# One block for router and experts, and a first expert round from the first four token tiles

## What is computed

```
x = x + g1 * mix                                  # output projection and residual
h = modulate(x, norm2_g, sh2, sc2)
lc = h @ router_c + b;  g_idx = argmax(lc)        # one of 4 groups
lf = h @ router_f + b;  lf_sel = the 4 values of that group
top_w, top_i = top_k(softmax(lf_sel), 2)          # two of its 4 experts
for e in range(16):
    hid = silu(h @ exp_gate[e]) * (h @ exp_up[e])
    out += combine[:, e] * (hid @ exp_down[e])
x = x + g2 * out
```

## Time and profile before

| | |
|---|---|
| three runs | 920.63, 917.87, 919.87 us, median 919.87 |
| profiled execution, span from first to last instruction | 917.0 us; its own time beside the span is not listed, the median of the runs lies 2.9 us above it |
| PE busy | 846.8 us, 92% |
| DVE, ACT, POOL busy | 47%, 27%, 8% |
| DMA, mean over the span | 249 GB/s |
| DMA in the slices from 596 us to 894 us | 304 to 425 GB/s a slice |
| mean granted PE clock | 0.958 of full |

### The profile page before, as it was taken

The page is one execution under the profiler, slowest core; times in us unless marked ns, Lnnn a source line. Parts: engine busy times, 40 slices in busy tenths (PEclk is TensorE's granted clock), DMA queues, the critical chain, the costliest instruction groups (busy, mean ns, idle before and its releaser), DMA issues. The chain is left out here.

```text
span 917.0 us, 18956 instructions
## 1 busy us (share of the span) xinstructions
PE 846.8 (92%) x8190; PEld 486.0 (53%) x8190; DVE 432.1 (47%) x878; ACT 249.9 (27%) x489; POOL 77.7 (8%) x126
## 2 busy tenths in 40 slices
PE   5999999999989987799988899928999999999998
PEld 4455555544656765688877555514344444333433
DVE  4321356222457877778885755661331000002248
ACT  5002222322588772323322302111111111111110
POOL 1180000000000002122211000120000000000040
PEclk9999999999999996899999799967999999999999
DMA  9989999573890001001322664299989999999993
GB/s 342 322 243 408 379 391 362 218 264 110 332 379 14 14 13 36 5 20 46 95 61 61 207 230 183 77 357 393 372 304 400 406 378 378 414 391 411 425 377 124
DMA packets 72612, 227.89 MB, mean 249 GB/s; under 512 B 10708, under 2 KB 15884, under 8 KB 66128
## 3 DMA queue, kind: packets, MB, share of 16 engines
q1 hardware_dynamic: 60784, 200.33, 58.6%
q10 hardware_dynamic: 7632, 14.64, 4.5%
q0 software_dynamic: 4112, 11.70, 3.8%
HBM read 166.98 MB, written 59.67 MB: 247 GB/s over the span
## 5 line engine op out<-in xcount | busy, mean ns | idle before, releaser
L2595 PE MATMUL ps<-arena 128*32 128x512 f32 (+2 forms) x800 | 170.2, 597 | 1.5 <-ACT arena L2730 1.5
L2595 PEld LDWEIGHTS ps<-arena 128*32 128x32 f32 (+2 forms) x800 | 61.3, 136 | 101.8 <-issue 99.1
L1012 PE MATMUL ps<-arena 128*128 128x128 f32 (+1 forms) x384 | 106.8, 435 | 0.0
L1012 PEld LDWEIGHTS ps<-arena 128*128 128x128 f32 x384 | 58.4, 190 | 50.6 <-issue 48.9
L2143 PE MATMUL ps<-arena 128*128 128x512 f32 x160 | 74.0, 615 | 1.9 <-PEq L1516 1.9
L2637 PE MATMUL ps<-arena 128*32 128x512 f32 (+2 forms) x352 | 70.6, 594 | 0.0
L748 DVE SCALAR_TENSOR_TENSOR arena<-arena 128x128 f32<-128x128 f32 (+3 forms) x56 | 30.9, 553 | 69.8 <-ACT arena L655 68.3
L2906 DVE TENSOR_TENSOR arena<-arena,ps 128x512 f32<-128x512 f32 x12 | 8.2, 687 | 100.3 <-ACT arena L2726 100.3
L891 PE MATMUL ps<-arena 128*128 128x512 f32 (+1 forms) x160 | 52.4, 486 | 0.0
L2143 PEld LDWEIGHTS ps<-arena 128*128 128x128 f32 x160 | 30.5, 197 | 37.3 <-issue 37.3
L2637 PEld LDWEIGHTS ps<-arena 128*32 128x32 f32 (+2 forms) x352 | 24.4, 132 | 38.7 <-issue 37.9
(11 more groups left out here) (395 smaller groups left out, 1315.1 us busy)
## 6 DMA issues: line engine op xcount, KB each, us to landing
gathered_tokens<-arena SPq DMA_DIRECT2D x16, 2560.0 KB, 21.2
arena<-in_exp_up_dram SPq DMA_DIRECT2D x16, 2048.0 KB, 20.8
arena<-in_exp_gate_dram SPq DMA_DIRECT2D x16, 2048.0 KB, 20.8
arena<-in_exp_down_dram SPq DMA_DIRECT2D x16, 2048.0 KB, 20.9
arena<-in_w_mod_dram SPq DMA_DIRECT2D x12, 2048.0 KB, 15.0
arena<-in_w_in_dram SPq DMA_DIRECT2D x4, 2048.0 KB, 12.5
expert_outputs<-arena ACTq DMA_DIRECT2D x10, 512.0 KB, 11.8
arena<-in_x_sample_dram SPq DMA_DIRECT2D x8, 512.0 KB, 9.1
```

Source lines behind the costliest of these rows:

```text
L1012: mm = pe.matmul(ps[:, b, 0:hi - lo], ring_of(what)[:, k, (e % 4) * P:(e % 4) * P + P], hT[:, k, lo:hi], start=(k == 0), stop=(k == KT - 1))
L2595: mm = pe.matmul(ps[c:c + m, b, :], xgT[:, k, c:c + m], w[n % 3][:, k, :], start=(k == 0), stop=(k == KT - 1))
```

## The change

The two blocks become one; each engine's two lists are joined. Besides:

- Round 0 takes 64 rows of each fixed place (two quarters and two quarters), round 1 the rest of both and the first quarter of place 2. Place 0 therefore stays until round 1. A round's results go to HBM in contiguous pieces (stretches), two each for rounds 0 and 1.
- Batches become tiles 0 to 2, tile 3, tile 4. After tile 3, the fixed experts' next row is set to at least 64 (first_rows), so that no row of tile 4 can fall in round 0.
- ACT loads round 0's rows when tiles 0 to 3 are scattered, in the middle of tile 4's routing; the rows of rounds 1 and 2 after tile 4's scatter and the table.
- PE turns round 0's rows ahead of the second half of tile 4's partial logits, and does tile 4's logits and ranks between the gate products of round 0.
- SP issues the gate weight of place 1 at attn_read, which PE sets when it has read the attention part of tile 4's projection; the down weight of place 1 follows the up weight; the weights of place 2 wait for the table, not for the block's end.
- DVE ranks the four values by comparing each with each (rank_of_four) in place of repeated maxima; the values for the softmax weights are made at the end (chosen_values).

```diff
-        SEGS = [[] for _ in range(NR)]
...
+        SEGS = [[(0, 0, 0, 2), (1, 2, 0, 2)], [(0, 0, 2, CAPQ[0] - 2), (1, CAPQ[0] - 2, 2, CAPQ[1] - 2)]] + [[] for _ in range(NR - 2)]
+        for n in range(len(FIXED), NE):
...
+        def stretches(r):
+            out = []
+            for n, c0, q0, nq in SEGS[r]:
+                at = QROWS * (sum(CAPQ[:n]) + q0)
+                if out and out[-1][1] + out[-1][2] == at:
+                    out[-1][2] += QROWS * nq
+                else:
+                    out.append([QROWS * c0, at, QROWS * nq])
+            return out
...
-        BATCHES = ((0, 2), (2, 4), (4, NTT))
+        BATCHES = ((0, 3), (3, 4), (4, NTT))
...
             @block.sync
             def _(sp):
...
-                sp.wait_ge(mix_mm, 2 * NTT - 1)
+                sp.wait_ge(attn_read, 1)
                 sp.dma_start(wg[1], exp_gate[0, FIXED[1]].rearrange("(p k) n -> p k n", p=P)).then_inc(ld_g[1], 16)
                 sp.wait_ge(mix_mm, 2 * NTT)
                 sp.dma_start(wu[1], exp_up[0, FIXED[1]].rearrange("(p k) n -> p k n", p=P)).then_inc(ld_u[1], 16)
-                sp.wait_ge(ld_g2b, 32)
+                sp.dma_start(wd[1], exp_down[0, FIXED[1]].rearrange("(p k) n -> p k n", p=P)).then_inc(ld_d[1], 16)
+                sp.wait_ge(h2_ok, NTT)
+                sp.wait_ge(table_ok, 1)
                 e = expert_at(sp, 2)
-                sp.dma_start(iota, consts[:, NCONST + 8 * C:]).then_inc(ld_iota, 16)
                 sp.dma_start(wg[2], gate_of(e)).then_inc(ld_g[2], 16)
                 sp.dma_start(wu[2], up_of(e)).then_inc(ld_u[2], 16)
-                sp.dma_start(wd[1], exp_down[0, FIXED[1]].rearrange("(p k) n -> p k n", p=P)).then_inc(ld_d[1], 16)
+                sp.dma_start(iota, consts[:, NCONST + 8 * C:]).then_inc(ld_iota, 16)
+                for b, (t0, t1) in enumerate(BATCHES):
+                    sp.wait_ge(scattered[b], 32 * (t1 - t0))
                 sp.dma_start(wd[2], down_of(e)).then_inc(ld_d[2], 16)
...
+                half_squares(4, 0)
+                act.wait_ge(scattered[0], 96)
+                act.wait_ge(scattered[1], 32)
+                load_rows(act, 0)
+                x2_turned(4, (0,))
+                half_squares(4, 1)
+                root_square(4)
+                x_out(0)
+                logits_out(4)
+                sigmoid(0)
+                act.wait_ge(scattered[2], 32)
+                act.wait_ge(table_ok, 1)
+                load_rows(act, 1)
+                load_rows(act, 2)
+                act.wait_ge(ec_ok, 1)
+                act.activation(expc, expc, ACT.Exp).then_inc(ex_ok, 1)
...
+                mix_half(4, 1, 0, (0, 1))
+                ranks(1)
+                mix_half(4, 1, 0, (2, 3))
+                pe.wait_ge(cat_ok, NTT)
+                mix_half(4, 0, 1)
+                mix_half(4, 1, 1)
+                x2_turn(4, (0,))
+                part_logits_of(4, (0,))
+                x2_turn(4, (1,))
...
                 x_turn(0)
-                gate_up(0)
+                part_logits_of(4, (1,))
+                pe.wait_ge(slot_ok, 2)
+                pe.wait_ge(xgT_ok, 1)
+                weights_landed(0, ld_g)
+                products(0, wg, GA, 0, 1)
+                logits_of(4)
+                products(0, wg, GA, 1, 5)
+                ranks(2)
+                products(0, wg, GA, 5, KT).then_inc(g6_mm, 1)
+                weights_landed(0, ld_u)
+                products(0, wu, UP, 0, KT).then_inc(u6_mm, 1)
                 x_turn(1)
                 h_turn(0)
+                pe.wait_ge(slot_ok, 3)
                 for r in range(1, NR):
...
+                def rank_of_four(n, ts, vals):
+                    for op, beside in ((ALU.is_equal, 0), (ALU.is_gt, 1)):
+                        ins = dve.tensor_tensor(beats[:, ts, :, beside], vals.unsqueeze(2).to_broadcast([P, n, 4, 4]),
+                                                vals.unsqueeze(3).to_broadcast([P, n, 4, 4]), op)
+                    ch(ins)
+                    ch(dve.tensor_tensor(beats[:, ts, :, 0], beats[:, ts, :, 0], earlier.unsqueeze(1).to_broadcast([P, n, 4, 4]), ALU.mult))
...
+                choose(1, *BATCHES[1])
+                place_rows(1)
+                ch(dve.tensor_tensor(offs[:, 4, 0:len(FIXED)], offs[:, 4, 0:len(FIXED)], first_rows, ALU.max))
```

More of the change, by code:

```diff
@@ L1947, in build, with stored_before @@
                 SEGS[r].append((n, lo - 4 * r, lo - at, hi - lo))
+        assert all(sum(nq for _, _, _, nq in one) == 4 for one in SEGS)
+        FIRST_ROUND = [min(r for r in range(NR) if n in [i for i, _, _, _ in SEGS[r]]) for n in range(NE)]
+        LAST_ROUND = [max(r for r in range(NR) if n in [i for i, _, _, _ in SEGS[r]]) for n in range(NE)]
+        def stretches(r):
[7 more added lines that the diff above has]
+            return out
+        def stored_before(r):
+            return 16 * sum(len(stretches(i)) for i in range(r))
         def load_rows(eng, r):
@@ L2513, in tiles_of @@
                 return [(0, P, SEGS[r][0][0])]
-            w = 64 if SEGS[r][0][3] == 2 else 32
+            w = 64 if all(nq == 2 for _, _, _, nq in SEGS[r]) else 32
             return [(QROWS * c, w, n) for n, c0, _, nq in SEGS[r] for c in range(c0, c0 + nq, w // QROWS)]
@@ new lines, in mix_half @@
+                def mix_half(tt, half, k4, js=range(NC4)):
+                    b = 2 + 2 * (tt % 2) + half
+                    for j in js:
+                        mm = pe.matmul(ps[:, b, :], catT[k4][:, j, tt * P:(tt + 1) * P], wout[:, half, NC4 * k4 + j, :],
+                                       start=(k4 == 0 and j == 0), stop=(k4 == 1 and j == NC4 - 1))
+                    if k4 and NC4 - 1 in js:
+                        mm.then_inc(mix_mm, 1)
+                    elif tt == NTT - 1 and half and NC4 - 1 in js:
+                        mm.then_inc(attn_read, 1)
@@ new lines, in _ @@
+                pe.wait_ge(ld_at, 64)
+                pe.wait_ge(ld_wout[0], 192)
+                mix_half(0, 0, 0)
+                mix_half(1, 0, 0)
+                turn(0)
+                turn(1)
+                pe.wait_ge(ld_wout[1], 48)
+                mix_half(0, 1, 0)
+                mix_half(1, 1, 0)
+                mix_rwkv(0)
+                turn(2)
+                mix_rwkv(1)
+                turn(3)
+                mix_attn(2)
+                turn(4)
+                mix_rwkv(2)
@@ L2585, in x_turn, with products, weights_landed @@
                     mm.then_inc(xgT_mm, 1)
+                def products(r, w, b, k0, k1):
+                    for k in range(k0, k1):
+                        for c, m, n in tiles_of(r):
+                            mm = pe.matmul(ps[c:c + m, b, :], xgT[:, k, c:c + m], w[n % 3][:, k, :], start=(k == 0), stop=(k == KT - 1))
+                    return mm
+                def weights_landed(r, landed_):
+                    for n, _, q0, _ in SEGS[r]:
+                        if q0 == 0:
+                            pe.wait_ge(landed_[n % 3], 16 * (n // 3 + 1))
                 def gate_up(r):
@@ L2929, in _ @@
                         y_out(r - 1)
+                dve.wait_ge(ld_g2b, 32)
                 early_sum(1)
```

943 lines of the change are left out of this document (449 added, 494 removed).

## The result

The changed kernel takes 930.2 us (median; 929.7 to 932.1) beside 919.8 of the kernel before on the same chip: 1.0139 times as long, 95% interval 1.0111 to 1.0168. Forecast were 925.9 us, with a range of 923 to 929: the sign was right, the size too small (+10.4 us where +6.0 was forecast). The profiled execution took 930.42 us, with a span of 928.6 where the one before had 917.0. (The time lies 1.8 to 1.9 us above the span in every execution that lists both. The traced execution of the kernel before thus took some 918.8 us, 1 us under its median, so the spans differ by 11.6 us and the medians by 10.4.)

A forecast was written before the change was run, and what follows sets the result against it. PE's hole until round 0's rows land was taken to bound the kernel through round 1's start, 641.9. Start +2.9 and second slow start +3.1 gave +6.0 us: 925.9, own range 923 to 929, whole range 912 to 931.

The forecast's parts named there:

- The signs named at the end of the prediction: Trace signs: slow tile 3 scatter, row load near 605, turn near 613, slow round 1 rows, 8 us PE hole before round 1.
- Up to X: Tile 3's scatter lands at 605.4, round 0's row load issues at 605.6, rows are turned at 613, 6.8 us earlier than before.
- X: The time PE turns round 0's rows: forecast 613, against 619.84 in the kernel before.
- From X to the issue of round 1's rows: Tile 4's routing inside round 0: logits X+5.4, row numbers X+12.3, scatters landed X+18.1, ACT issues round 1's rows at X+18.3.
- I take 10.4: Round 1's row load beside expert 2's weights takes 10.4 us (ends 3.3 and 12.7), landing at X+28.7.
- The second slow start: PE's clock falls in the hole before round 1, whose products take 17.0 us instead of 13.9: +3.1 us.
- What follows: After round 1, a lagging weight stream and other side work cost 0, with 0 to 2 us kept for the range.
- the 1.8 us to spare: In a later round, the up weight landing at 781.1 is wanted at 782.9 by its products.
- All clear: Rival: both scatters and both row loads land at their lone prices; round 1 starts at 627.2, -14.7, 905.2 us; chance 0.13.
- Only the second load is clear: Rival: X = 613, round 1's rows after 4.7 us, PE keeps its clock; start 638.2, -3.7, 916.2 us; chance 0.12.

The follow-up runs named there:

- D: Distance from PE's first turn for the last tile (kernel before: from the projection's end) to the end of round 1's products, in one trace; changed kernel 68.7 us.
- the wait for all three weights: Changed kernel, with gate, up and down weight 2 issued only when round 1's rows have landed: 930.23 us, a single execution.
- the run with round 2's rows moved: Changed kernel, with ACT loading round 2's rows only after it has copied round 1's turned rows: 933.93 us, a single execution.

## Why the prediction was right or wrong

**What bounds, the two holes, the sign: right.** The signs named at the end of the prediction came: a tile 3 scatter of about 10 us, PE's turn near 613 (614.72), round 1's rows less than 3 us behind the weights and over 9 on the way, a hole before round 1 (12 us for the 8) with the clock down behind it. Only ACT's load of round 0's rows came sooner, at 601 instead of 605.

**Up to X: right by two errors that nearly cancel.** The scatters were issued 1.5 us sooner than I put them (589.95 and 591.21) and landed after 9.9 us, not 12.7: at 601.1, not 605.4. But the rows of round 0 then took 13.6 us to PE's turn where the sum had 7.4, because at 601 more of the 6.3 MB was still to come. X is 614.7, not 613: +1.7. The rule used there, that the rows finish when the weights run out, was the sound part: down weight 1, the last of the three (issued at 597.62, 17.3 us on the way), landed at 614.9 where I had 612 for the end of the weights.

**From X to the issue of round 1's rows: right.** Logits at X+5.0, row numbers X+11.9 (forecast X+12.3), scatters landed X+17.0 (forecast X+18.1): -1.3 us at the issue.

**The term that failed is "I take 10.4" for round 1's rows.** It measured 15.7: +5.3 us. It was taken from one load of 10.6 us, issued in one piece of 128 rows. Round 1's comes in three, of 64, 32 and 32 rows, the third 2.2 us behind the first (its address is read from the plan), and has three weights beside it. The single runs give the parts: 4.5 us without weights, about 7.5 more for the first, about 3 more for the other two. The upper end that I kept, 12.7, was for a scatter, and the third piece alone took 13.5.

I had also taken the pace of the row that was nearest, 0.35 MB in 4 us, which is 0.09 MB a us; here it was 0.05. Both stretches share by packets, nearly one to one, but the packets went slower here (99 of the weights in 6 us, 88 in 4 us before). This goes with the shape of the pieces, and the trace of the kernel before shows it. Its stretches beside that one piece of 128 rows, and beside round 3's load, which ACT issued at 641.82 and 643.10 in two pieces of 64 rows (columns as in the earlier trace rows):

```profile
628.00:632.00 4.00, 4.00 (x9) 1.67 (x8) 0.00 (x0) 0.00 (x0) 0.00 (x0) 0.88 0.99 420
646.00:654.00 8.00, 8.00 (x80) 2.39 (x76) 0.69 (x1) 0.60 (x1) 0.00 (x0) 1.00 1.02 284
```

The DMA engines were as busy, but moved 284 GB/s instead of 420; in the changed kernel it is 301 from 640 to 645. Those two pieces took 9.7 and 11.3 us, 12.6 from the first issue to the last landing, for the same 512 KB. So a row of the right shape was there, and it was 2 us dearer than the one taken. Why small pieces slow the weights beside them no run tells, and none loads round 1 in one piece.

**The second slow start: over-sized.** The clock fell as forecast, but it was back by 655, some 2.7 us into round 1's products where it was 6.1 before, and they took 15.2 us and not 17.0. Why it came back sooner is open.

The sum with measured terms: +1.7 - 1.3 + 5.3 makes round 1 start 5.7 us later than forecast (650.5 against 644.8), and -1.8 for the shorter slow start leaves +3.9 on the forecast +6.0: 9.9, as measured.

**What follows: right for the change, and wrong for the best rival.** No later round waits for a weight after the change, so 0 was right. But the 1.8 us to spare was read as a limit on delay only. It also limits gain: with D 16.9 us shorter than before, the up weight took 7.9 back. The rival "All clear", priced at 905.2, would by this hardly have come to that.

**The rivals.** "Only the second load is clear" is what the wait for all three weights made, and it did not give 916: it overlooked that round 1 needs gate weight 2 as well as its rows. The lone prices of "All clear" themselves held: 3.6 and 4.1 us for round 0's two pieces of 256 KB where no weight ran, against 10.5 and 13.0 in the changed kernel. A scatter with no weight beside it took 3.3 to 3.5; the 4.2 of the earlier trace rows was not paid on nearly empty engines, since the scatter before it in that queue was on its way until 615.1 and those of the second batch until 613.9. The Trainium skill gives its fit for one transfer ("DMA: Bandwidth & Descriptors", section "Anatomy of one DMA"), 2.0 us plus bytes over 436 GB/s, for transfers that GpSimd starts. For the half megabyte of a scatter that is an estimate of 3.2 us, 0.1 to 0.3 under the scatters without weights. Carried over to ACT's pieces of 256 KB, which that section does not speak of, it would be an estimate of 2.6 us, 1.0 to 1.5 under the lone pieces and a quarter to a fifth of those beside weights.

## What to carry to other kernels

A small transfer on the critical path is priced by what is in flight beside it, not by its size: here 4.5, 12 or 15.7 us for the same rows, and a weight that nobody needs yet is what makes the difference. Moving the weight behind the rows only pays if the next product does not need that weight too, and moving the issue earlier, so that other products cover the slow load, gave back 14.5 us with the weights in their old order. Read a price from a load of the same shape: here one piece of 128 rows was taken for three smaller ones. Before counting a gain at one place, read who has the least to spare further on: what was won here beyond some 7 us came back as a wait for one weight 130 us later.

## What was not expected of the hardware

Queues that compete move nearly equal numbers of packets (99 to 97, 66 to 63), so the one with the smaller packets gets the smaller share of bytes. Beside row loads in pieces of 64 or 32 rows the DMA engines moved 284 and 301 GB/s, beside one of 128 rows 420, at the same busy share. Putting the rows in the weights' queue does not help by itself: behind one 2 MB weight they took 11.5 and 11.7 us, nearly as long as beside it (12.1 and 12.5). And the same hole of 12.2 us on PE was followed by products that began at the lower clock in the changed kernel (15.23 us; the clock is back at 653.2, 2.7 us into them) and by products at full pace in the run with round 2's rows moved (13.94; 0.55 in the 3.1 us ahead of them, 1.00 from their start); what makes the difference is open.
